# First projection: six tiles instead of four are multiplied undivided and divided afterwards

## What is computed

```python
def rmsnorm(x, w):
    xf = x.astype(jnp.float32)
    y = xf * lax.rsqrt(jnp.mean(xf * xf, axis=-1, keepdims=True) + RMS_EPS)
    return (y * w.astype(jnp.float32)).astype(x.dtype)

h = rmsnorm(h_res, norm1_w[l])
proj = h @ w_in[l]
(q, k, v, z, b_raw, a_raw, sc_b, sc_c, sc_x, gate_a, gate_b) = jnp.split(proj, SPLIT_POINTS, axis=-1)
# in gated_deltanet_bidir:
qkv = jax.nn.silu(depthwise_conv_centred(jnp.concatenate([q, k, v], axis=-1), conv_w))
g = -jnp.exp(A_log) * jax.nn.softplus(a_raw.reshape(Bsz, L, 2, DN_HEADS) + dt_bias)
```

## Time and profile before

| | us |
|---|---|
| median of 3 runs | 1632.62 |
| lowest and highest | 1632.46, 1635.77 |
| the profiled execution | 1633.61 |
| its span in the trace | 1631.8 |
| TensorE busy with products | 1604.4 |
| VectorE busy | 970.5 |
| GpSimd busy | 960.2 |
| ScalarE busy | 784.6 |

### The profile page before, as it was taken

One profiled execution on the slowest core, in us unless ns is written; L12 is line 12 of the kernel. 1 busy time (PEld: TensorE's weight loads), 2 busy tenths in 40 slices (PEclk: granted clock), 3 DMA queues, 4 the chain that ended last, 5 costly groups with the idle time before them and its releaser, 6 DMA issues.

```text
span 1631.8 us, 25962 instructions
## 1 busy us (share of the span) xinstructions
PE 1604.4 (98%) x10257; PEld 1418.9 (87%) x10257; DVE 970.5 (59%) x1731; ACT 784.6 (48%) x1219; POOL 960.2 (59%) x537
## 2 busy tenths in 40 slices
PE   7999999999999999999999999999999999999998
PEld 7999988898999888889999998888888888888887
DVE  7778955844443001257777771238999972457744
ACT  6666544333333222257666653336544463366652
POOL 3455645333456445547888874449978665466661
PEclk9999989999999999999999999999999999999999
DMA  5586289464423334333333333333333323233332
GB/s 193 155 276 190 85 247 283 141 183 152 149 77 96 94 98 147 98 90 95 107 104 105 108 112 104 105 102 93 101 93 104 117 88 104 91 101 93 104 103 78
DMA packets 128704, 202.61 MB, mean 124 GB/s; under 512 B 33328, under 2 KB 74440, under 8 KB 128584
## 3 DMA queue, kind: packets, MB, share of 16 engines
q1 hardware_dynamic: 126248, 197.46, 40.0%
q10 hardware_dynamic: 2336, 3.51, 0.6%
HBM read 170.97 MB, written 29.97 MB: 123 GB/s over the span
## 4 chain that ended last, share of the span: by engine, by line
PE 86%; DVE 8%; ACT 2%; issue 1%; POOL 1%; DMA 1%; DVEq 0%; SPq 0%; ACTq 0%
PE ps L478 62%; PE ps L571 12%; PE ps L2140 4%; DVE cacc L2668 3%; DVE inv L877 1%; DVE prd L874 1%; PE ps L1185 1%; PE ps L1199 1%; PE ps L1193 1%; PE ps L1206 1%; PE ps L1210 1%; POOL hp L3039 1%; PE ps L1152 1%; PE ps L1171 1%; DMA x_in<-in_x 0%
## 5 line engine op out<-in xcount | busy, mean ns | idle before, releaser
L466 POOL TENSOR_TENSOR w_lo<-w_raw,w_hi 128x1024 fp32r<-128x1024 f32 x220 | 528.5, 2409 | 410.7 <-ACT w_hi L460 398.2
L478 PE MATMUL ps<-hp,w_hi 128*128 128x268 f32 (+2 forms) x1728 | 378.0, 326 | 0.0
L478 PEld LDWEIGHTS ps<-hp,w_hi 128*128 128x128 f32 x1728 | 269.8, 189 | 26.2 <-issue 2.2
L460 ACT ACTIVATE w_hi<-w_raw 128x1024 fp32r<-128x1024 f32 x220 | 230.7, 1054 | 124.0 <-DMA w_raw<-in_w 116.2
L478 PE MATMUL ps<-hp,w_lo 128*128 128x268 f32 (+2 forms) x864 | 233.6, 323 | 0.0
L547 POOL TENSOR_TENSOR g_lo<-g_raw,g_hi 128x896 fp32r<-128x896 f32 x88 | 188.1, 2140 | 41.2 <-ACT g_hi L541 41.2
L478 PE MATMUL ps<-n_hi,w_hi 128*128 128x512 f32 x464 | 180.7, 389 | 0.0
L478 PE MATMUL ps<-n_hi,w_lo 128*128 128x512 f32 x464 | 180.5, 389 | 0.0
L478 PE MATMUL ps<-n_lo,w_hi 128*128 128x512 f32 x464 | 180.5, 389 | 0.0
L571 PE MATMUL ps<-b_lo,g_hi 128*128 128x256 f32 x616 | 173.9, 282 | 0.0
L1568 DVE SCALAR_TENSOR_TENSOR ps<-u_in,par,ps 128x511 f32<-128x511 f32 (+14 forms) x210 | 154.6, 739 | 6.5
(11 more groups left out here) (481 smaller groups left out, 3285.5 us busy)
## 6 DMA issues: line engine op xcount, KB each, us to landing
w_raw<-in_w SPq DMA_DIRECT2D x220, 512.0 KB, 3.6
g_raw<-in_wg SPq DMA_DIRECT2D x88, 256.0 KB, 2.6
d_y<-zero SPq DMA_DIRECT2D x6, 688.0 KB, 6.2
d_x<-zero SPq DMA_DIRECT2D x6, 688.0 KB, 6.5
d_at<-at SPq DMA_DIRECT2D x16, 256.0 KB, 3.3
d_kc<-kc SPq DMA_DIRECT2D x16, 256.0 KB, 3.3
d_qd<-eg SPq DMA_DIRECT2D x16, 256.0 KB, 3.2
d_p<-dec SPq DMA_DIRECT2D x16, 256.0 KB, 3.5
```

What stands on the lines that cost most here:

```text
L460: e.activation(w_hi[:, lies(u), :], w_raw[:, lies(u), :], ACT.Copy).then_inc(s_hi, 1)
L466: e.tensor_tensor(w_lo[:, lies(u), :], w_raw[:, lies(u), :], w_hi[:, lies(u), :].bitcast(F32), ALU.subtract).then_inc(s_lo, 1)
L478: mm = e.matmul(ov, w, r[:, k, t0:t1], start=(first and n == 0 and p3 == 0), stop=(last and n == len(tiles) - 1 and p3 == 2))
```

## The change

Tiles 4 and 5 are multiplied from the undivided rows, as tiles 0 to 3 are, and VectorE divides their results in the banks. Tile 6 becomes the first tile on the divided rows and takes over the order by slices. The taps of tiles 4 and 5 wait for the division. VectorE's two new instructions stand at the end of its part of tiles 3 and 4, ahead of the side tasks of these tiles.

```diff
-        fd = Signal(sem("s_fold"), n1=5, n2=16, gu=6 * FT, down=KT, n3=6, lr=2 * LT)
+        fd = Signal(sem("s_fold"), n1=7, n2=16, gu=6 * FT, down=KT, n3=6, lr=2 * LT)
...
-                elif n == 4:
+                elif n == 6:
                     e.wait_ge(*cv.at("t", 4 * (n - 1)))
                     gemm_hi(e, n, tile_out(n), TAP5, hp_hi, K8, ready=lambda k: hi.at("n1", k + 1))
                     gemm_lo(e, n, tile_out(n), TAP5, hp_lo, K8, ready=lambda k: lo.at("n1", k + 1)).then_inc(s_pe, 1)
                 elif 2 <= n < len(TILES):
                     e.wait_ge(*cv.at("t", 4 * (n - 1)))
-                    gemm(e, n, tile_out(n), TAP5, *((u_hi, u_lo) if n < 4 else (hp_hi, hp_lo)), K8).then_inc(s_pe, 1)
+                    gemm(e, n, tile_out(n), TAP5, *((u_hi, u_lo) if n < 6 else (hp_hi, hp_lo)), K8).then_inc(s_pe, 1)
...
-                e.wait_ge(*(fd.at("n1", (1, 2, 4, 5)[n]) if n < 4 else (s_pe, n + 1)))
+                e.wait_ge(*(fd.at("n1", (1, 2, 4, 5, 6, 7)[n]) if n < 6 else (s_pe, n + 1)))
...
                     scaled(3)
+                if n in (3, 4):
+                    scaled(n + 1)
                 for task, arg in SIDE.get(n, ()):
```

## The result

The median after is 1638.85 us (7 runs, 1637.91 to 1639.92) against 1632.62 us (7 runs) on the same chip: a ratio of 1.003, 95% interval 1.0021 to 1.004. A second set of 11 runs of the changed kernel (`e11_after_again`) gave 1638.05 us against 1634.26 us, 1.0027 (1.0018 to 1.0036). By these ratios the change makes the kernel slower by 4.4 to 4.9 us. (A ratio and its interval are worked out from the single runs; it can differ from the quotient of two medians, here by up to 0.0008. The medians differ by 6.2 and 3.8 us.) The profiled execution of after took 1639.39 us with a span of 1637.6 us.

A forecast was written before the change was run, and what follows sets the result against it. TensorE, 98% busy, was taken as the bound, with VectorE's chain deciding from tile 4's taps to `dk`. Span 1631.8 + 2.72 (delay) + 1.0 (clock) = 1635.5, time 1637.3, median forecast 1636.3 us, range 1633.8 to 1639.5.

The forecast's parts named there:

- TensorE's part: Tiles 4 and 5: tile 4's wait and slower start go, 0.95 us; TensorE some 1.05 us ahead without anything else.
- The first division: Ahead of tile 4's taps: runs in VectorE's 1.59 us of idle time; taps start at 51.75 instead of 51.91.
- The second division: Behind tile 4's taps: VectorE waits for the end of tile 5, so the key copies start 2.72 us later.
- From the copies to `gdec`: VectorE's rows from 55.00 to 66.40: no idle time gives the delay back, so `gdec` is 2.72 us late.
- TensorE's three waits: Ahead of `kt` 1 (about 1.5 us), `ktm` and `dk` (2.7 us): all end in `dk`'s start, +2.72 us together.
- The clock: At `dk`, `gr` and tile 7: a longer weak stretch brings more half clock, +1.0 us, from -1.5 to +2.2.
- The rival with all of them at half clock: All of `dk` and `gr` may run at half clock, up to +3.7 us; time 1639.0 us, chance 0.09.
- Nothing given back: Behind tile 7: later TensorE waits move along with the delay, 0 us given back, 2.7 as the bound.

The follow-up runs named there:

- e11_after_again: The changed kernel itself, unaltered, run once more for a second trace and ratio; 1638.05 us, ratio 1.0027 to before.
- e2_five_tiles: The changed kernel with tile 5 back on the divided rows, so only tile 4 is undivided in addition; 1634.69 us, ratio 1.0008 to before.
- e1_gda_ahead: The changed kernel with VectorE doing `gda` ahead of the second division and the first key copies; 1633.93 us, ratio 1.0001 to before.
- e4_split8_behind_gda: The changed kernel with GpSimd's split of tile 8's weights waiting until VectorE has finished `gda`; 1635.12 us, ratio 1.0006 to before.
- e3_tile5_only: The changed kernel with tile 4 back on the divided rows, so only tile 5 is undivided in addition; 1639.72 us, ratio 1.0033 to before.
- e5_before_split7: The kernel before with GpSimd's split of tile 7's weights waiting until VectorE has finished `gda`; 1632.07 us, ratio 0.9989 to before.

## Why the prediction was right, and where it was off

The time forecast was 1636.3 us (1633.8 to 1639.5), the median 1638.85: slower, by the mechanism that was named as the likeliest, inside the range, with a sum of +3.7 where the traces show +4.6. The median lies only 0.65 us below the upper end of the range. By its steps:

- **TensorE's part.** Right in size: tile 4 takes 49.30 - 43.21 = 6.09 us (6.06 forecast), and tile 5 is signalled 0.03 us from the place worked out for it. That this lead would not count was right too, and `e2_five_tiles` shows it alone.
- **The first division.** Right: it lies in the idle time, and the taps start at 51.00; 51.75 less 0.76 is 50.99.
- **The second division.** Right: VectorE idles 2.18 us (about 2.1 forecast), and the copies are 2.76 us late (2.72). `e1_gda_ahead` shows that this wait is the cause: the order alone brings the kernel back to 1.0001.
- **From the copies to `gdec`.** Here a term was left out. The prediction took the rows between 55.00 and 66.40 as fixed work, since there is no idle time between them. Some 1.9 us of them was a hold by GpSimd, counted as busy time of L1593 (56.20, 2.05 us long). It became 0.36 us longer, and it could as well have gone: `e4_split8_behind_gda` has `gdec` 2.24 us sooner than after, counted from tile 3's taps. `gdec` was 3.11 us late, not 2.72.
- **TensorE's three waits.** Right: 1.50 us ahead of `kt` 1 (about 1.5), 0.69 us ahead of `ktm` (0.5, the difference of 66.1 and 65.61), 2.62 us ahead of `dk` (2.7), and they do not add.
- **The clock.** Right in place, with some luck, and too small: +1.0 was taken from -1.5 to +2.2, +1.51 was measured. The clock fell at about 70.6, with 3.73 - (70.6 - 69.04) = 2.2 us of `dk` and `gr` still to come, the very 2.2 us of the prediction. They took 3.8 us, 1.7 times as long, not the 1.45 times that +1.0 stands for; tile 7 was 0.1 us faster. No row of before had these products at half clock; now `dk`'s four products take 1.06 us instead of 0.63, and `gr`'s 32 take 1.94 instead of 1.15. The rival with all of them at half clock is what `e3_tile5_only` does: 6.44 us for `dk` and `gr`, so its price was 2.7 and not 3.7. The luck is in the place: the prediction let the clock fall as far behind the end of tile 6 as in before, 5.3 us, and in after it was 5.4 us. In other traces it was 2.4 us (`e3_tile5_only`), 3.2 us (`e5_before_split7`), 4.1 us (`e2_five_tiles`) and 4.9 us (`e4_split8_behind_gda`), so this distance is no constant.
- **Nothing given back.** Right: A + B is +4.61 us, tile 15's tap 4.55 us late, and the ratios stand for 4.4 to 4.9 us.

The sum that was missing: 2.76 + 0.35 + 1.51 = 4.62 us, 0.9 us over the forecast's 3.72. The other 1.65 us of the distance to 1638.85 belong to no step that a trace shows. The base is a likely place: the forecast stands on a median of 1632.62, while before had medians of 1634.13 to 1634.42 in the later comparisons (27 to 33 runs each), and 1634.26 + 4.62 is 1638.9.

## What to carry to other kernels

A step that is added to an engine that works in order costs what stands behind it the whole time until its operand is there, not its own duration: here 0.63 us of work cost 2.76 us, and one move in the list, of work that did not need that operand, brought the kernel back to 1.0001. Time saved on the busiest engine ahead of a wait that another engine ends is turned into a longer wait, and a longer wait can cost clock behind it as well, so price the two together. Busy rows without a gap are not yet fixed work: compare each short instruction with others of its form, since one that takes ten times as long can be a wait of another kind.

## What had not been expected of the hardware

GpSimd can hold VectorE. Instructions of 128x80 elements that take 0.19 to 0.24 us took 2.04 to 2.47 us when they met a 2.4 us subtraction of GpSimd that had started first, and ended within 0.1 us of its end: L1593, L1597 or L1599, one in each of eleven traces, and one of L1607 in three of these. Two other forms were not held. A reciprocal of before (L2853, one input), which started at 1091.11 us, 0.16 us behind a split, took 0.18 us, as another one did at 1093.90 with no split beside it. The taps, which read the banks (`ps`) and one tensor of SBUF (the memory in which the other tensors lie), took 0.77 us each beside a split, as without one. The Trainium skill (SBUF — State Buffer, Who interferes with whom) says that VectorE and GpSimd share a pair of SBUF ports, which goes whole to the one that starts first, and that on VectorE instructions with two SBUF inputs and certain copies and scalar forms need it. The traces agree for the instructions named here: the held ones are of these forms, and the reciprocal and the taps are not.

At half clock the short decay products took 1.7 times their time, and ten unread products in the wait ahead of them, 2.60 us of work that did not delay them (A +3.09 against +3.10), were worth 2.97 us behind it.
